# A decoder layer with a routed mixture of experts: in the expert loop VectorE transposes the next rows before it reads the gate and up projections, and works out the slots of a later item only after the activations

## What is computed

```python
logits = h @ w_router + b_router                      # 512 tokens, 32 experts
top_val, top_exp = top_k(logits, 4); w = softmax(top_val)
for each token and each of its 4 experts e:
    gt = minimum(x @ w_gate[e] + b_gate[e], 7)
    up = clip(x @ w_up[e] + b_up[e], -7, 7)
    y += w * ((gt * sigmoid(1.702 * gt) * (up + 1)) @ w_down[e] + b_down[e])
x = layer_norm(alpha * x + (1 + g2) * y)
```

## Time and profile before

| | |
|---|---|
| median of three runs | 1671.43 us (1670.47 to 1671.85) |
| the profiled execution | 1670.47 us, of which 1668.3 us are the span of its instructions |
| TensorE matmuls | 1390.9 us busy, 83% of the span |
| VectorE | 800.4 us, 48% |
| ScalarE / GpSimd | 199.0 us / 284.4 us |
| HBM read | 474.40 MB, mean 293 GB/s over the span, about 406 GB/s where loads are back to back |
| expert loop | from about 503 us to 1645 us of the span |

### The profile page before, as it was taken

One profiled execution on the slowest core, in us unless ns is written; L12 is line 12 of the kernel. 1 busy time (PEld: TensorE's weight loads), 2 busy tenths in 40 slices (PEclk: granted clock), 3 DMA queues, 4 the chain that ended last, 5 costly groups with the idle time before them and its releaser, 6 DMA issues. The chain is left out here.

```text
span 1668.3 us, 38820 instructions
## 1 busy us (share of the span) xinstructions
PE 1390.9 (83%) x13037; PEld 571.8 (34%) x13038; DVE 800.4 (48%) x2816; ACT 199.0 (12%) x522; POOL 284.4 (17%) x217
## 2 busy tenths in 40 slices
PE   6999988889838976678886998697999996969683
PEld 3444445454423321222221333232333331323131
DVE  1139675554964521433442554454455553525345
ACT  1011255550010000000000000000000000000002
POOL 0000000113422210111111222121122221212111
PEclk9999979989959977778987999898899997979787
DMA  9821066824174999999999889889989969496994
GB/s 342 213 76 51 5 214 228 241 85 177 67 297 161 396 407 414 407 409 410 406 361 409 299 320 406 323 323 385 403 320 404 390 229 408 120 407 223 405 410 153
DMA packets 161041, 488.14 MB, mean 293 GB/s; under 512 B 39791, under 2 KB 58283, under 8 KB 143596
## 3 DMA queue, kind: packets, MB, share of 16 engines
q1 hardware_dynamic: 144876, 470.84, 72.9%
q0 software_dynamic: 16128, 16.82, 5.0%
HBM read 474.40 MB, written 17.76 MB: 295 GB/s over the span
## 5 line engine op out<-in xcount | busy, mean ns | idle before, releaser
L1044 PE MATMUL banks<-arena,misc 128*32 128x512 f32 x5248 | 666.8, 638 | 177.1 <-DMA arena<-in_w_up 128.1
L1044 PEld LDWEIGHTS banks<-arena,misc 128*32 128x32 f32 x5248 | 164.2, 113 | 573.2 <-DMA arena<-in_w_up 306.9
L1054 PE MATMUL banks<-arena,master 128*32 128x256 f32 x5248 | 330.2, 394 | 4.5 <-DVE master L1703 2.1
L1784 DVE TENSOR_SCALAR cst<-banks 128x256 f32<-128x256 f32 x82 | 34.8, 425 | 425.9 <-PE banks L1044 423.1
L1054 PEld LDWEIGHTS banks<-arena,master 128*32 128x32 f32 x5248 | 169.3, 114 | 156.3 <-issue 71.5
L649 POOL DMA_INDIRECT misc<-moe_input,misc x84 | 88.3, 1052 | 729.3 <-DVE misc L1728 686.3
L665 POOL DMA_INDIRECT moe_output<-misc x82 | 130.2, 1587 | 228.4 <-issue 224.6
L1275 ACT ACTIVATE banks<-cst 128x256 f32<-128x256 f32 x82 | 31.8, 387 | 1089.9 <-DVE cst L1784 1089.9
L814 PE MATMUL banks<-arena 128*128 128x512 f32 x256 | 112.6, 595 | 0.0
L1708 DVE TENSOR_SCALAR master<-cbias 128x128 bf16<-128x128 f32 x340 | 95.1, 344 | 12.8 <-issue 6.5
L1747 DVE LOAD_MASK_SELECT banks<-master x84 | 1.2, 14 | 169.7 <-DMA master<-expert_bias 158.6
(11 more groups left out here) (307 smaller groups left out, 1130.3 us busy)
## 6 DMA issues: line engine op xcount, KB each, us to landing
arena<-in_w_gate SPq DMA_DIRECT2D x256, 512.0 KB
arena<-in_w_up SPq DMA_DIRECT2D x256, 512.0 KB
arena<-in_w_down SPq DMA_DIRECT2D x128, 1024.0 KB
arena<-in_w_ada SPq DMA_DIRECT2D x12, 2048.0 KB, 13.1
arena<-in_x SPq DMA_DIRECT2D x2, 2048.0 KB, 8.7
arena<-in_w_in SPq DMA_DIRECT2D x2, 2048.0 KB, 9.7
master<-bias_by_distance SPq DMA_DIRECT2D x16, 256.0 KB, 4.6
arena<-in_w_in SPq DMA_DIRECT2D x8, 256.0 KB, 4.3
```

The source lines that it names most:

```text
L1044: last = nc.tensor.matmul(two(bank[2 * b][strip(j), :]), hTe[:, k, :], arena[:, 24 * b + 2 * k:24 * b + 2 * k + 2, quarter(j)], start=Fals ...
L1054: last = nc.tensor.matmul(bank[2 * b + 1][strip(j), 0:256], actT[:, q, c, :], DN(b, q, c)[:, quarter(j)], start=False, stop=(q == 3 and c ...
```

## The change

Five calls in VectorE's `body` change places. `rows_transposed` goes from behind the two clamps to the very front, ahead of both. `moved_on` and `slot_values` go from behind the transposition to behind `down_bias`, ahead of `one_hot`. Nothing is added or removed, and the other engines' programs are as they were.

```diff
                 dve.wait_ge(s_a, m + 1)
+                rows_transposed(here)
                 dve.wait_ge(s_pr, m + 1)
                 nc.vector.tensor_scalar(gcl, bank[2 * b][:, 0:256], 7.0, None, ALU.min).then_inc(s_gdr, 1)
                 dve.wait_ge(s_act, m + 1)
                 nc.vector.tensor_scalar(ucl, bank[2 * b][:, 256:512], 7.0, -7.0, ALU.min, ALU.max).then_inc(s_urd, 1)
-                rows_transposed(here)
-                moved_on(m + 2, m + 2, m * 2 + 4, m + 1)
-                slot_values(m + 3, m * 2 + 5)
                 dve.wait_ge(s_gdr, m + 1)
                 dve.wait_ge(s_sig, m + 1)
                 nc.vector.tensor_tensor(gcl, sig, gcl, ALU.mult).then_inc(s_pr, 1)
...
                 nc.vector.scalar_tensor_tensor(gcl, ucl, 1.0, gcl, ALU.add, ALU.mult).then_inc(s_act, 1)
                 activations_transposed(m + 2, m + 1)
                 down_bias(b, bias_landed, m + 1)
+                moved_on(m + 2, m + 2, m * 2 + 4, m + 1)
+                slot_values(m + 3, m * 2 + 5)
                 one_hot(expert_of(ds(m + 3, 1)))
                 scatter_indices(m + 3, landed)
```

## The result

The changed kernel takes 1684.44 us (median of 5 runs, 1681.13 to 1687.54); the kernel before takes 1670.47 us (median of 5, 1667.83 to 1671.85). Ratio 1.0088, interval [1.0072, 1.0105]: 14 us slower, where 3.5 us were forecast. The profiled execution took 1679.86 us with a span of 1677.7 us, 9.4 us over that of before. It is the fastest of the changed kernel's executions; a second profile of the same kernel (the repeated run among the experiments) has a span of 1684.4 us.

A forecast was written before the change was run, and what follows sets the result against it. The loop was taken as bound by weight DMA in some stretches, by TensorE in others. First item -0.7, loop +3.3 and end +0.9 gave +3.5 us on the median 1671.43: 1674.9 us, range 1670.8 to 1681.5 us.

The forecast's parts named there:

- the mechanism and its place: TensorE-bound items with weights moving: later indices delay the gather, so the transposition waits for it; 0.32 us per item.
- the 4.27 us to the indices: VectorE, from the transposition's start at the item's front to the gather's indices ready: 4.27 us, instead of 2.10.
- the 0.95 us to the gather: GpSimd starts the gather 0.95 us behind its indices, at 5.22 us into the item instead of 3.05.
- the slack of 0.87 us: Lateness of the transposition absorbed before TensorE loses time: 0.67 us from its earlier start plus 0.2 us true slack.
- -0.7 us at the first item: First item, no `down` to cover the transposition: TensorE starts 0.67 us earlier, total -0.7 us.
- +0.9 us at the end: Kernel's end: the last weighting waits for the scatter before it, which starts 0.8 to 1.0 us later; +0.9 us.
- the loop's term: Expert loop: chains of loaded items cost 2.4 us, one gather late on GpSimd +0.9; +3.3 us, bounds 0 to about +10.
- the landing: Gather's issue to last packet: 2.5 us in quiet items, mean 5.35 us for the slow 67 of 81 gathers.
- ring: Transposition, indices, gather, landing, next transposition: 8.1 us before, 10.97 us after, against TensorE's 10.65 us per item.
- The ring stays inside: Rival: the real ring is 10.65 us or less, only the ends -0.7 + 0.9 are left; 1671.6 us; chance 0.3.
- The ring costs much: Rival: slower issue beside `one_hot` or longer packet waits, 0.3 us more per turn, loop loses about 10 us; 1681.5 us; 0.15.
- Faster: Rival: early transposition shortens 9 TensorE waits by 0.67 us each, 6.0 us off; 1665.4 us; chance 0.07.

The follow-up runs named there:

- the repeated run: The changed kernel once more, unaltered, for a second trace, timed against the kernel before: 1684.96 us, ratio 1.0080.
- held loads: Expert's load held after bias row and first half block until TensorE used four more blocks: changed kernel 1681.45 us, kernel before 1680.41 us; unheld kernel before 1671.04 us.

## Why the prediction was wrong, point by point

**Right:** the mechanism and its place; the 4.27 us to the indices (4.23 measured), the 0.95 us to the gather (0.94), the slack of 0.87 us (0.8); -0.7 us at the first item (-0.66) and +0.9 us at the end (+1.1, and +0.6 in the second trace); the 0 to 0.2 us for the gather's issue beside `one_hot` (1.11 instead of 1.05 us); no cost in quiet items, which stay at 10.64 us; activations and clamps of no account; that TensorE's waits for the transposition behind a bias row give nothing back.

**Wrong: the size of the loop's term**, +3.3 us, where the two traces show +11.6 and +16.7 us (loop from the first item's last gate/up matmul to the last item's: 1120.1 us before, 1131.0 and 1136.1 after, and 0.66 won at the first item). The failed step is the landing: I took every gather's landing time as it was in the kernel before ("67 of the 81 in the loop are of the slow kind, 4.8 to 5.74 us, mean 5.35") and the quiet ones as quiet. A transfer moved by 2.2 us past another queue's issue doesn't keep its landing time. 12 gathers (18 in the second trace) now take 5.9 us or more, and chains that I let start with 0.87 us in hand start with little or none: by the estimate above the loop's term is 6 us with the old landing times (a ring 0.1 us longer than forecast, and both gathers that started late on GpSimd counted instead of one), and 18 and 22 us with the new ones. SyncE's queue in the trace of before had it: its first block is at 976.60, between the gather's old place at 975.33 and its new one at 977.5. With held loads, where that race is mostly undone, the change costs 1.0 us, against 13.9 us without, though waits for weights hide part of the cost there. The rest is small: 0.5 instead of 0.4 us from landing to transposition, and 5.4 to 5.5 instead of 5.35 us for the other loaded gathers.

**The rivals.** "The ring stays inside" fell with the 45 waits. "The ring costs much" came nearest: about +10 us by slower issue beside `one_hot`, which is 0.06 us, or by packets that wait longer, which is what happened, though by 2.6 to 4.3 us in eight gathers behind the start of a load and not by 0.3 us in each turn. I gave it 0.15. "Faster" fell: with the transposition alone moved there was no gain that can be told from none. That the block after the first wasn't there yet fits this, and no run shows it by itself. The fixed cost in DMA: Bandwidth & Descriptors of the Trainium skill (the part on where a transfer's fixed cost goes) gives an estimate of 2.3 us for this gather; that fits the quiet ones (2.5 us) and none beside weights.

## What to carry to other kernels

When a step that issues a transfer is moved, its landing time isn't moved with it: look in the trace for what other queues issue between the old place and the new one, and read the landing time of a transfer issued behind that. Write down the whole loop from a buffer's release over its refill to its next use, and compare it with the period of the engine that sets the time; above that period each item pays, but even below it (10.3 us here, against 10.65) single late transfers can cost if the consumer has little slack. Work that starts another engine's transfer belongs into the shadow of a wait (here the sigmoid's) and not behind the work that follows it.

## What the runs showed of the hardware that I had not expected

A gather of 48 packets from the software queue lands in 2.3 to 3.3 us if it is issued before the first weights, in about 4 us with half a block (0.5 MB) ahead, in 5.7 to 7.4 us just behind 1 MB or more of a load that starts on quiet DMA engines, and mostly in 5.0 to 5.7 us in the middle of a long load (up to 6.2 us in the changed kernel's two traces). Where one load follows another without a break, its start is no worse: 5.4 us for the changed kernel's gathers of 1009.9 and 1268.4. So the start of a load after a quiet time is the worst moment. DMA: Bandwidth & Descriptors of the Trainium skill (the part on queues, rings and completion order) says that each DMA engine takes turns between queues, a packet at a time; with three packets per engine, as the profile counts them, that would let a gather through within a few packets of weights, which take 0.17 us each on average there. The trace doesn't agree for the gather as a whole: that of 975.92 in the changed kernel has only 32 of its 48 packets started by 981.0 us, and the first of them starts 4.1 us after the issue. No run here shows what the gather waits for until its first packet.
